# Two attention stages of the second block rewritten: scores from high and low halves on 32-row and 64-row tiles

## The chip, the cores and the metric

The kernel runs on one core of a Trainium2 chip. The metric is the device time of one launch in microseconds (us). The core has five engines that matter here: TensorE (PE), VectorE (DVE), ScalarE (ACT), GpSimd (POOL), and SyncE (SP), which issues the weight loads.

## The reference, cut to what matters

Two transformer blocks of two layers each work on 512 tokens of width 1024. The change touches the second block, which also carries 256 context tokens. In each layer four mixers write a quarter of the width each; two of them are attentions with 4 heads of 64:

```python
# neighbourhood attention: query r,q sees the keys of its window, and all 256 context keys
s_loc = einsum('brqhd,brikhd->bhrqik', qg, k_band) * scale + bias   # outside the window: -inf
s_ctx = einsum('brqhd,blhd->bhrql', qg, k_ctx) * scale
p = softmax(concatenate([s_loc, s_ctx]))
# differential attention: each head has two halves of 32 columns, rotated (rope) for the 512 tokens
p = softmax(q1 @ k1.T * scale) - lam * softmax(q2 @ k2.T * scale)   # over 512 + 256 keys
o = p @ v ; y = rms_norm(o, g) * (1 - lam_init)
```

In layer 0 the 256 context tokens are queries too (over the context keys alone); in layer 1 they only give keys and values. All is float32.

## The kernel before, in words

Each engine has its own instruction list in one fixed order; semaphores join them. Names of work: `("S", u)` is the score tile of unit u. A unit is (kind, layer, head pair j, block q of 128 queries, head h). Kinds are "n" and "d" (the 512 tokens in neighbourhood and differential attention: 16 units a layer) and "nc" and "dc" (context queries: 8 units, layer 0 only).

PSUM has 8 banks: `PB` is a ring of six, taken in turn, whose next taker waits until the last user of that bank is done; `PO` is a ring of two, in which a head pair's output gathers over its query blocks. SBUF rings (`PR` probabilities, `PT` transposed probabilities, `BM` bias tiles, 2 slots, `QR`, `TA`) work the same way.

**Neighbourhood attention** (`B["na", l]`). The keys lie in `KZ`, per head a 128-row tile in which the other head's 64 rows are zero, so a score is a plain 128-row float32 matmul of 512 columns and one of 256. Per unit: PE scores `S` and `Sc`; DVE adds the bias tile with a scalar_tensor_tensor (`na_top`), ACT copies `Sc` beside it, DVE takes the maximum over 768, ACT the exponential, DVE the reciprocal and a multiply of all 768 (`share`); PE transposes (`turn`, 3 units later), ACT copies the transposes (`keys_down`), PE multiplies with V (`values`, 5 units later). `out_proj(2)`, the output projection of the mixer before, is laid between the first units, two of its 8 column tiles at each of iterations 1 to 4. POOL makes the bias tiles in its own loop, in which `fetch(n + 1)` waits until DVE has used tile n - 1 and then issues two DMAs, and the next wait is for the DMAs of tile n:

```python
for n in range(len(us)):
    if n + 1 < len(us):
        fetch(n + 1)
    eng.wait_ge(*after(("bl", us[n])))
    b = S["BM"].get(us[n])
    eng.tensor_tensor(b, b, S["MASK"], ADD).then_inc(*done(("bm", us[n])))
```

**Differential attention** (`B["df", l]`). The head pairs are two sequences, j = 0 then j = 1. For each: PE projects q and k, ACT copies them (`QR`), PE multiplies with the rotation matrix, POOL and DVE join the parts (`rope`), DVE writes k as four zero-padded tiles of 128 rows (`KZ`, 4 additions on 32 rows); only then come the units. Per unit: four score tiles (two halves, each 512 and 256 keys, in a bank each), `df_top` with four reduces, a join and a scaling, `df_one` with four exponentials, `df_share` with a reciprocal, a multiply of 768 and a scalar_tensor_tensor of 768, then `turn`, `keys_down`, `values` as above with lags of 2 and 3. `out_proj(1)` is laid into iterations 1 to 4 of j = 0. After each j: squares, a sum on PE, logarithm and exponential on ACT, three Newton steps and a product on DVE. Then `out_proj(3)`.

The first block's grouped attention (`gqa_score`, `attend_blocks`) already works on pairs of units: high and low halves in the type fp32r, three products on 64-row tiles, the two heads in turn, unscaled probabilities, and one scaling of the output (`shares`, `out_scaled`).

Of the kernel before, what the change touches and what calls it, by code (L numbers as in the profile page):

```python
# [25 lines left out]
F32 = mybir.dt.float32  # L26
# [5 lines left out]
P = 128  # L32
D = 1024
KD = D // P
T = 512
# [48 lines left out]
def constants():  # L84
# [60 lines left out]
    mask = np.where(inside, 0.0, -1e30).astype(f)  # L145
# [99 lines left out]
class Ring:  # L245
# [13 lines left out]

    def get(self, key):  # L260
        known = self.steps.known
        return self.slots[0 if known is None else known[("slot", self.name, key)]]

# [4 lines left out]
def build(nc, A, known):  # L268

    ctx = ExitStack()  # L270
    with ctx:
# [39 lines left out]
        banks = [ctx.enter_context(nc.psum_tensor(f"bank_{i}", [P, 512], F32)) for i in range(8)]  # L311
# [38 lines left out]
        PB = Ring(st, "PB", [b[:, :] for b in banks[0:6]])  # L350
        PO = Ring(st, "PO", [b[:, :] for b in banks[6:8]])
# [125 lines left out]
        def common(c, tag, sq=3, sums=1):  # L477

            return dict(SQ=c.ring("SQ" + tag, sq, T), Y=c.ring("Y" + tag, 2, T), N=c(T), AC=c.ring("AC" + tag, sums, T))
# [3 lines left out]
        def attention(c, tag, nk, p_slots, t_slots):  # L483
            return dict(PR=c.ring("PR" + tag, p_slots, nk), PT=c.ring("PT" + tag, t_slots, nk // P, P),
                        ST=c.ring("ST" + tag, 6, 16))

        def paired(c, tag, nk, p_slots, t_slots):
            return dict(RB=c.ring("RB" + tag, 1, T), RS=c.ring("RS" + tag, 3, 8), PR=c.ring("PR" + tag, p_slots, nk),
# [43 lines left out]
        for l in range(L):  # L532
# [12 lines left out]
            b = dict(H=H, YG=Y2, Q=c(2, T + CT), KZ=c(4, T + CT), V=c(6, 256), MASK=c(T), BM=c.ring("BM" + t, 2, T), **com)  # L545
            b.update(attention(c, t, T + CT, 4, 5))
# [3 lines left out]
            b = dict(H=H, YG=Y2, Q=c(T + CT), KZ=c(4, T + CT), V=c(6, 256), TAB=c(2, T),  # L550
                     QR=c.ring("QR" + t, 1, T), TA=c.ring("TA" + t, 1, T), TBB=c(T), **com)
            b.update(attention(c, t, T + CT, 4, 4))
# [28 lines left out]
        def na_units(l):  # L581
            return units("n", l, range(2), TB) + (units("nc", l, range(2), 2) if l == 0 else [])

        def df_units(l, j):
            return units("d", l, [j], TB) + (units("dc", l, [j], 2) if l == 0 else [])
# [27 lines left out]
        def _(eng):  # L613
# [70 lines left out]
            def turn(u, S, blocks, ready="p"):  # L684

                eng.wait_ge(*after((ready, u)))
                pk = (u, 0) if u[0] in ("d", "dc") else u
                p = S["PR"].get(pk)
# [60 lines left out]
            def attend(us, S, score, V, blocks, okey, nq, between=None, turn_lag=TURN, value_lag=VALUES):  # L749

                for i in range(len(us) + value_lag):
                    if between:
                        between(i)
# [1814 lines left out]
```

## Time and profile before

| | us |
|---|---|
| median of 3 runs (lowest, highest) | 3548.5 (3540.64, 3551.41) |
| the profiled execution, its own time | 3541.35 |
| its span | 3539.6 |
| neighbourhood attention from its first score, layer 0 and 1 | 91.05 and 76.8 |
| differential attention from its first projection to `out_proj(3)`, layer 0 and 1 | 214.75 and 185.4 |

A launch is one pass through the stages. The four stretches in the last two lines are what the change rewrites; their sum is 568 us, 16% of the span. The granted clock of TensorE is given as a share of 2.4 GHz.

### The profile page before, as it was taken

The numbers are of one execution on the slowest core, as the hardware profiler recorded it, in microseconds if no ns is written. First come the engines' busy times: TensorE is split into PE (matmuls) and PEld (weight loads), VectorE is DVE, ScalarE is ACT, GpSimd is POOL, SyncE is SP. The second block draws the span as 40 slices with busy tenths as digits, with TensorE's granted clock in tenths as the row PEclk, the third lists the DMA queues.
The fourth block names the chain that finished last, engine by engine and source line by source line (L and its number), as shares of the span: only waits on it lengthen the run. The fifth ranks groups of instructions, "written<-read, shape, count | busy, mean of one in ns | idle before, by whom it ended". The sixth has DMA issues, their size and how long they took to land.

```text
span 3539.6 us, 38820 instructions
## 1 busy us (share of the span) xinstructions
PE 3237.2 (91%) x15536; PEld 2082.1 (59%) x15536; DVE 1327.0 (37%) x2224; ACT 1012.4 (29%) x1976; POOL 233.2 (7%) x224
## 2 busy tenths in 40 slices
PE   7999979998999979988999878999999998869998
PEld 3555644534555545433666446888788565448886
DVE  2452231223552322121433754333323333563444
ACT  2452211111551211123123444222222222343332
POOL 0010000000000100000022001000001022000000
PEclk9999989998999989998999999999999999989999
DMA  4011238871002248885210001333232210013221
GB/s 165 25 37 49 72 120 356 357 323 50 35 25 78 77 200 336 366 343 211 71 36 25 13 1 72 119 119 119 109 118 76 99 41 26 1 61 105 97 95 48
DMA packets 62001, 413.62 MB, mean 117 GB/s; under 512 B 7504, under 2 KB 8016, under 8 KB 14464
## 3 DMA queue, kind: packets, MB, share of 16 engines
q1 hardware_dynamic: 55664, 392.06, 28.7%
q0 software_dynamic: 5008, 16.98, 1.4%
q8 instruction: 126, 2.06, 0.2%
q10 hardware_dynamic: 1152, 2.10, 0.2%
q14 instruction: 51, 0.42, 0.0%
HBM read 409.01 MB, written 2.10 MB: 116 GB/s over the span
## 4 chain that ended last, share of the span: by engine, by line
PE 85%; DVE 8%; ACT 3%; issue 2%; POOL 1%; DMA 1%; DVEq 0%; ACTq 0%; SPq 0%; POOLq 0%
PE bank L644 82%; PE bank L645 3%; DVE arena L1798 3%; ACT arena L1292 3%; DVE x L1798 1%; DMA weight<-in_ada_w 0%; POOL arena L2471 0%; POOL arena L2481 0%; POOL arena L2413 0%; DVE arena L2031 0%; DVE arena L2333 0%; DVE arena L2029 0%; DVE tokens_low L1798 0%; DMA weight<-in_w_up 0%; DVE arena L2049 0%
## 5 line engine op out<-in xcount | busy, mean ns | idle before, releaser
L644 PE MATMUL bank<-arena,weight 128*128 128x512 f32 (+2 forms) x2080 | 826.4, 555 | 59.1 <-DVE arena L1798 42.0
L1292 ACT ACTIVATE arena<-bank 128x512 f32<-128x512 f32 (+5 forms) x746 | 374.5, 520 | 1690.2 <-PE bank L644 1394.7
L644 PE MATMUL bank<-arena 128*64 128x128 f32 (+4 forms) x3888 | 620.6, 342 | 54.7 <-ACT arena L1292 23.7
L644 PEld LDWEIGHTS bank<-arena,weight 128*128 128x128 f32 (+1 forms) x2080 | 392.7, 191 | 469.9 <-issue 427.5
L644 PE MATMUL bank<-weight,arena 128*64 128x512 f32 (+5 forms) x2936 | 608.8, 530 | 33.0 <-ACT arena L1292 9.7
L644 PEld LDWEIGHTS bank<-arena 128*128 128x128 f32 (+2 forms) x3888 | 399.7, 170 | 238.5 <-issue 142.8
L644 PEld LDWEIGHTS bank<-weight,arena 128*64 128x64 f32 (+2 forms) x2936 | 294.9, 150 | 316.2 <-issue 261.3
L644 PE MATMUL bank<-hidden,weight_part 128*128 128x512 f32 (+1 forms) x2304 | 446.4, 355 | 0.0
L644 PE MATMUL bank<-tokens_high,weight_part 128*128 128x512 f32 (+1 forms) x1536 | 420.6, 359 | 23.9 <-DVE tokens_low L1798 23.7
L644 PEld LDWEIGHTS bank<-hidden,weight_part 128*128 128x128 f32 x2304 | 381.1, 189 | 70.3 <-DVE arena L1798 3.5
L644 PEld LDWEIGHTS bank<-tokens_high,weight_part 128*128 128x128 f32 x1536 | 276.5, 191 | 82.7 <-DVE tokens_low L1798 30.4
L644 PE MATMUL bank<-tokens_low,weight_part 128*128 128x512 f32 (+1 forms) x768 | 274.4, 357 | 0.0
L645 PE MATMUL bank<-mats,arena 128*128 128x128 f32 (+1 forms) x1232 | 176.9, 280 | 69.7 <-DVE arena L1798 26.4
L2413 POOL TENSOR_TENSOR arena<-arena 128x512 f32<-128x512 f32 x72 | 85.0, 1180 | 2098.4 <-ACT arena L1292 2096.7
L1798 DVE SCALAR_TENSOR_TENSOR x<-bank,arena,x 128x512 f32<-128x512 f32 x192 | 142.8, 748 | 200.1 <-PE bank L644 199.5
L645 PEld LDWEIGHTS bank<-mats,arena 128*128 128x128 f32 (+1 forms) x1232 | 143.0, 143 | 127.1 <-DVE arena L1798 44.0
L1292 ACT ACTIVATE weight_part<-weight 128x2048 fp32r<-128x2048 f32 x64 | 122.1, 1908 | 325.6 <-PE bank L644 322.1
L1292 ACT ACTIVATE arena<-bank,arena 128x512 f32<-128x512 f32 (+1 forms) x312 | 185.5, 608 | 71.1 <-DVE arena L2298 49.4
L1798 DVE SCALAR_TENSOR_TENSOR arena<-arena 128x512 f32<-128x512 f32 (+5 forms) x177 | 109.9, 628 | 211.0 <-ACT arena L1292 207.2
L1292 ACT ACTIVATE arena<-arena 128x512 f32<-128x512 f32 (+4 forms) x264 | 163.3, 631 | 66.4 <-DVE arena L2256 40.9
L2357 DVE TENSOR_TENSOR weight_part<-weight,weight_part 128x2048 fp32r<-128x2048 f32 x64 | 146.7, 2292 | 91.6 <-ACT weight_part L1292 88.3
L1834 DVE TENSOR_REDUCE arena<-bank 128x1 f32<-128x512 f32 (+1 forms) x160 | 98.0, 634 | 211.2 <-PE bank L644 207.4
(115 smaller groups left out, 1676.7 us busy)
## 6 DMA issues: line engine op xcount, KB each, us to landing
weight<-in_w_gate SPq DMA_DIRECT2D x64, 1024.0 KB, 13.8
weight<-in_w_up SPq DMA_DIRECT2D x64, 1024.0 KB, 6.7
weight<-in_w_down SPq DMA_DIRECT2D x64, 1024.0 KB, 10.1
weight<-in_w_ff SPq DMA_DIRECT2D x64, 1024.0 KB, 5.0
weight<-in_ada_w SPq DMA_DIRECT2D x48, 1024.0 KB, 5.5
weight<-in_w_in SPq DMA_DIRECT2D x26, 1024.0 KB, 6.1
weight<-in_w_o SPq DMA_DIRECT2D x8, 1024.0 KB, 4.8
weight<-in_w_mem_kv SPq DMA_DIRECT2D x8, 1024.0 KB, 4.8
```

The lines of the kernel that those rows point to most:

```text
L644: mm = lambda o, a, b, first=True, last=True: eng.matmul(o, a, b, start=first, stop=last, skip_group_check=True)
L645: tr = lambda o, a, rows=P: eng.transpose(o, a, mat("ident", rows, rows))
L1292: act = lambda o, i, f=ACT.Copy, **k: eng.activation(o, i, f, **k)
L1798: stt = lambda o, a, s, b, p, q: eng.scalar_tensor_tensor(out=o, in0=a, scalar=s, in1=b, op0=p, op1=q)
L1834: eng.tensor_reduce(s[:, 0:1], PB.get(("S", u))[:, 0:n], AX, MAX, negate=True).then_inc(*done(("nb", u)))
L2357: tt(b, weights[slot_of[key]][:, :], a, SUB).then_inc(*done(("split", key), WF(key)))
L2413: eng.tensor_tensor(a, a, S["SQ"].get((tag, k))[:, 0:n], ADD).then_inc(*done(S["SQ"].free((tag, k)), *((("summed", tag),) if k == KD - 2 e ...
```

## The change

**Scores.** q and k are written as a high part in the type fp32r (`high`, on ACT) and a low part (`low`, on DVE), and a score is the sum of high x high, high x low and low x high. In neighbourhood attention (`na_score`) the two heads of a pair lie in rows 0 to 63 and 64 to 127 and their products follow each other in turn; the loop is `attend_blocks`, in which an iteration is a pair of units and `out_proj(2)` lies in iterations 1 to 4 of these. In differential attention (`df_score`) each half of a head lies in 32 rows, and the six products of one half (512 and 256 keys, three parts) follow each other into two neighbouring banks of `PB` (`take_pair`), so that DVE and ACT read 768 keys at once; the transposes of a unit take such a pair too (`turn_wide`).

**Order.** Both head pairs of differential attention are projected and rotated first, and their units are one sequence. The sums of squares of the first head pair come six iterations after its last unit.

**Softmax.** In neighbourhood attention `tensor_tensor_reduce` adds the bias and takes the minimum of the negated score in one instruction, for 512 and for 256 keys; the probabilities stay unscaled, and the output is divided by the sums (`shares`, `out_scaled`); DVE copies the transposes of each second head. In differential attention `p = p1 + s * p2` needs one pass of 768, and the output is divided afterwards.

POOL's loop over the bias tiles keeps its order, its two slots and its two DMAs a tile. The zero-fills of `KZ` are gone. The diff, cut to its core (PE first, then ACT, DVE and POOL):

```diff
+    def take_pair(self, key):
+
+        self.n += self.n % 2
+        slot = self.n % len(self.slots)
+        self.n += 2
+        formers = [self.free(self.owner[i]) for i in (slot, slot + 1) if i in self.owner]
+        self.owner[slot] = self.owner[slot + 1] = key
+        self.steps.put(("slot", self.name, key), slot)
+        return self.pairs[slot // 2], formers
...
+PB = Ring(st, "PB", banks[0:6])
+PB.pairs = [p[:, :] for p in pairs[0:3]]
...
-    b = dict(H=H, YG=Y2, Q=c(2, T + CT), KZ=c(4, T + CT), V=c(6, 256), MASK=c(T), BM=c.ring("BM" + t, 2, T), **com)
-    b.update(attention(c, t, T + CT, 4, 5))
+    b = dict(H=H, YG=Y2, **{n: c.rounded(f"na_{n}{l}", 2, T + CT) for n in ("QH", "QL", "KH", "KL")}, V=c(6, 256),
+             MASK=com["AC"].slots[0], ZERO=com["AC"].slots[1][:, 0:1], BM=Ring(st, "BM" + t, com["SQ"].slots), **com)
+    b.update(paired(c, t, T + CT, 4, (2, 2), [com["N"]]))
...
-    b = dict(H=H, YG=Y2, Q=c(T + CT), KZ=c(4, T + CT), V=c(6, 256), TAB=c(2, T),
-             QR=c.ring("QR" + t, 1, T), TA=c.ring("TA" + t, 1, T), TBB=c(T), **com)
...
+    b = dict(H=H, YG=Y2, **{n: c.rounded(f"df_{n}{l}", 2, T + CT) for n in ("QH", "QL", "KH", "KL")}, V=c(6, 256), TAB=com["SUMS"],
+             QR=Ring(st, "QR" + t, com["SQ"].slots), TA=c.ring("TA" + t, 1, T), TBB=c(T), **com)
+    b.update(RB=c.ring("RB" + t, 1, T), RS=c.ring("RS" + t, 3, 8), PR=c.ring("PR" + t, 4, T + CT),
+             PT=c.ring("PT" + t, 3, 6, P), ST=c.ring("ST" + t, 6, 8))
...
+    def turn_wide(u, S, blocks):
+
+        eng.wait_ge(*after(("p", u)))
+        p = S["PR"].get((u, 0))
+        o, formers = PB.take_pair(("T", u))
+        for former in formers:
+            eng.wait_ge(*after(former))
+        for c in range(blocks):
+            i = tr(o[:, c * P:(c + 1) * P], p[:, c * P:(c + 1) * P])
+        i.then_inc(*done(("out", ("T", u)), S["PR"].free((u, 0))))
...
-        def na_score(u):
-            kind, _, j, q, h = u
...
-                tile(("S", u), [S["Q"][:, j, q * P:q * P + P]], [z[:, 0:T]])
-                tile(("Sc", u), [S["Q"][:, j, q * P:q * P + P]], [z[:, T:T + CT]], n=CT)
...
-        attend(na_units(l), S, na_score,
...
+        def na_score(pu):
...
+            for name, keys in (("S", slice(0, T)), ("Sc", slice(T, T + CT))):
...
+                o = [take_bank((name, u)) for u in heads_of(pu)]
+                for n, (a, b) in enumerate((("QH", "KH"), ("QH", "KL"), ("QL", "KH"))):
+                    for h in range(2):
+                        r = slice(64 * h, 64 * h + 64)
+                        i = mm(o[h][:, 0:keys.stop - keys.start], S[a][r, j, at:at + P], S[b][r, j, keys], n == 0, n == 2)
...
+        attend_blocks(na_blocks(l), S, na_score,
...
-        def df_score(u):
+        def df_score(u, half):
             kind, _, j, q, h = u
-            for half in range(2):
-                z = S["KZ"][:, 2 * h + half, :]
...
+            o, formers = PB.take_pair(("S", u, half))
+            for former in formers:
+                eng.wait_ge(*after(former))
+            z = 2 * h + half
+            r = slice(32 * z, 32 * z + 32)
...
+            for n, (a, b) in enumerate((("QH", "KH"), ("QH", "KL"), ("QL", "KH"))):
+                lhs = S[a][r, j, at:at + P]
                 if kind == "d":
-                    lhs = [S["Q"][:, q * P:q * P + P]]
-                    tile(("S", u, half), lhs, [z[:, 0:T]])
-                    tile(("Sc", u, half), lhs, [z[:, T:T + CT]], n=CT)
...
+                    mm(o[:, 0:T], lhs, S[b][r, j, 0:T], n == 0, n == 2)
+                c = T if kind == "d" else 0
+                i = mm(o[:, c:c + CT], lhs, S[b][r, j, T:T + CT], n == 0, n == 2)
...
+        project("dq", "w_dq", [0], both, True, wdq)
+        project("dk", "w_dk", [0], True, True, wdk)
+        df_turn("dq", 0)
+        project("dq", "w_dq", [1], both, True, wdq)
+        df_turn("dk", 0)
+        project("dk", "w_dk", [1], True, True, wdk)
+        df_turn("dq", 1)
+        us = df_units(l)
+        for i in range(len(us) + DF_LAG + 1):
+            if i == 0:
+                df_turn("dk", 1)
+            beside(1)(i)
+            if i == len(us) // 2 + DF_POST:
+                df_norm(0)
+            if i < len(us):
+                df_score(us[i], 0)
+            if DF_LAG <= i < len(us) + DF_LAG:
+                u = us[i - DF_LAG]
+                turn_wide(u, S, 6 if u[0] == "d" else 2)
+            if i < len(us):
+                df_score(us[i], 1)
+            if DF_LAG < i and us[i - DF_LAG - 1][4] == 1:
+                u = us[i - DF_LAG - 1]
+                values([u[:4] + (h,) for h in range(2)], S,
...
+                if df_ends(u):
+                    shares(df_okey(u), S, u[3] + 1, 2)
+        df_norm(1)
...
+        def high(dst, key, scale, j, i):
...
+            act(S[dst][:, j, cols], PB.get(key)[:, 0:(T, CT)[i]], scale=scale).then_inc(*done((key[0] + "h", l, j, i)))
...
-        def na_soft(u):
...
-            act(p[:, T:T + CT], PB.get(("Sc", u))[:, 0:CT], ACT.Copy, scale=64 ** -0.5).then_inc(*done(PB.free(("Sc", u)), ("sc", u)))
...
-            act(p, p, ACT.Exp, bias=s[:, 1:2], accum_out=s[:, 2:3]).then_inc(*done(("e", u)))
...
+        def na_exps(pu):
...
+            for u in heads_of(pu):
+                eng.wait_ge(*after(("nb", u)))
+                p, at = S["PR"].get(u), 2 * pu[3] + u[4]
+                src = p if pu[0] == "n" else PB.get(("Sc", u))[:, 0:CT]
+                act(p if pu[0] == "n" else p[:, 0:CT], src, ACT.Exp, bias=S["ST"].get(u)[:, 0:1], scale=-1.0,
+                    accum_out=r[:, at:at + 1]).then_inc(*done(*((PB.free(("Sc", u)),) if pu[0] == "nc" else ()), S["ST"].free(u), ("e", u)))
...
-                    act(p[:, 0:T], PB.get(("S", u, half)), ACT.Exp, bias=b, scale=32 ** -0.5, accum_out=s[:, 6 + 2 * half:7 + 2 * half]).then_inc(*done(PB.free(("S", u, half))))
-                    act(p[:, T:T + CT], PB.get(("Sc", u, half))[:, 0:CT], ACT.Exp, bias=b, scale=32 ** -0.5, accum_out=s[:, 7 + 2 * half:8 + 2 * half]).then_inc(*done(PB.free(("Sc", u, half)), *((("e", u),) if half else ())))
...
-            squares(("od", l, j), S, [PO.get(("od", l, j))])
...
+        def df_exp(u, half):
...
+            act(p[:, 0:n], PB.get_pair(("S", u, half))[:, 0:n], ACT.Exp, bias=s[:, half:half + 1],
+                accum_out=total).then_inc(*done(PB.free(("S", u, half)), ("e", u, half)))
...
+        def df_down(u):
...
+            act(pt[:, 0:n, :], PB.get_pair(("T", u))[:, 0:n * P].rearrange("p (c q) -> p c q", c=n)).then_inc(*done(PB.free(("T", u)), ("pt", u, 0)))
...
+            if i < len(us):
+                df_exp(us[i], 0)
+            if DF_LAG <= i < len(us) + DF_LAG:
+                df_down(us[i - DF_LAG])
+            if i < len(us):
+                df_exp(us[i], 1)
+            if DF_LAG < i and df_ends(us[i - DF_LAG - 1]):
+                u = us[i - DF_LAG - 1]
+                shares(df_okey(u), S, u[3] + 1)
...
+        def low(dst, high, key, scale, j, i):
...
+            stt(S[dst][:, j, cols], PB.get(key)[:, 0:(T, CT)[i]], scale, S[high][:, j, cols], MUL, SUB).then_inc(*done(PB.free(key), (key[0] + "l", l, j, i)))
...
-            stt(p[:, 0:T], PB.get(("S", u)), 64 ** -0.5, S["BM"].get(u), MUL, ADD).then_inc(*done(PB.free(("S", u)), S["BM"].free(u), ("pr0", u)))
...
-            eng.tensor_reduce(s[:, 0:1], p, AX, MAX).then_inc(*done())
-            eng.wait_ge(vector_step, done.count)
-            ts(s[:, 1:2], s[:, 0:1], -1.0, None, MUL).then_inc(*done(("nb", u)))
...
+        def na_tops(pu):
+            for u in heads_of(pu):
...
+                eng.wait_ge(*after(("out", ("S", u))))
+                eng.wait_ge(*after(("bm", u)))
+                eng.tensor_tensor_reduce(p[:, 0:T], PB.get(("S", u)), S["BM"].get(u), 1.0, 3.0e38, ADD, ALU.min,
+                                         s[:, 0:1]).then_inc(*done(PB.free(("S", u)), S["BM"].free(u)))
+                eng.wait_ge(vector_step, done.count)
+                eng.wait_ge(*after(("out", ("Sc", u))))
+                eng.tensor_tensor_reduce(p[:, T:T + CT], PB.get(("Sc", u))[:, 0:CT], S["ZERO"].broadcast_to([P, CT]), 1.0, s[:, 0:1], ADD, ALU.min,
+                                         s[:, 0:1]).then_inc(*done(PB.free(("Sc", u)), ("nb", u)))
...
-                    eng.tensor_reduce(s[:, 2 * half:2 * half + 1], PB.get(("S", u, half)), AX, MAX).then_inc(*done())
...
-                eng.tensor_reduce(s[:, 10:12], s[:, 0:4].rearrange("p (a b) -> p a b", a=2), AX, MAX).then_inc(*done())
-                eng.wait_ge(vector_step, done.count)
-                ts(s[:, 4:6], s[:, 10:12], -(32 ** -0.5), None, MUL).then_inc(*done(("nb", u)))
...
-                eng.reciprocal(s[:, 14:16], s[:, 12:14]).then_inc(*done())
...
-            tt(s[:, 15:16], s[:, 15:16], LAM[l][:, 4:5], MUL).then_inc(*done())
...
-            ts(p, p, s[:, 14:15], None, MUL).then_inc(*done())
-            eng.wait_ge(vector_step, done.count)
-            stt(p, q, s[:, 15:16], p, MUL, ADD).then_inc(*done(("p", u), S["ST"].free(u), S["PR"].free((u, 1))))
...
-                tt(S["KZ"][r, z, 0:T], S["TA"].get(rkey)[r, :], S["TBB"][r, :], ADD).then_inc(*done(*((S["TA"].free(rkey), S["QR"].free(rkey), ("dkc", l, j, 0)) if z == 3 else ())))
...
+            eng.wait_ge(*after(("ta", (l, n, j))))
+            tt(a, a, S["TBB"], ADD).then_inc(*done(("drope", l, n, j), S["QR"].free((l, n, j))))
...
+            tt(low[:, j, 0:T], S["TA"].get((l, n, j)), high[:, j, 0:T], SUB).then_inc(*done((n + "l", l, j, 0), S["TA"].free((l, n, j))))
...
+        def df_top(u, half):
...
+            eng.tensor_reduce(s[:, half:half + 1], PB.get_pair(key)[:, 0:T + CT if u[0] == "d" else CT], AX, MAX, negate=True).then_inc(*done(("nb", u, half)))
...
+        def df_join(u):
...
+            eng.wait_ge(*after(("e", u, 1)))
+            eng.reciprocal(s[:, 3:4], s[:, 2:3]).then_inc(*done())
+            eng.wait_ge(vector_step, done.count)
+            stt(s[:, 4:5], s[:, 3:4], S["RS"].get(df_okey(u))[:, at:at + 1], LAM[l][:, 4:5], MUL, MUL).then_inc(*done())
+            eng.wait_ge(vector_step, done.count)
+            p, q = S["PR"].get((u, 0))[:, 0:n], S["PR"].get((u, 1))[:, 0:n]
+            stt(p, q, s[:, 4:5], p, MUL, ADD).then_inc(*done(("p", u), S["ST"].free(u), S["PR"].free((u, 1))))
...
+        for n, j in tiles4:
+            df_rope(n, j)
+            df_low(n, j)
+        us = df_units(l)
+        for i in range(len(us) + DF_LAG + 2):
+            beside(1)(i)
+            if i < len(us):
+                df_top(us[i], 0)
+            if 1 <= i <= len(us):
+                u = us[i - 1]
+                df_join(u)
+                if df_ends(u):
+                    shares(df_okey(u), S, [])
+            if i == len(us) // 2 + DF_POST:
+                df_post(0)
+            if i < len(us):
+                df_top(us[i], 1)
+            if DF_LAG + 1 < i and df_ends(us[i - DF_LAG - 2]):
+                u = us[i - DF_LAG - 2]
...
-        eng.memset(S["KZ"], 0.0).then_inc(*done(("nz", l)))
...
-            eng.tensor_tensor(b, b, S["MASK"], ADD).then_inc(*done(("bm", us[n])))
+            eng.tensor_tensor(b, S["MASK"], b, SUB).then_inc(*done(("bm", us[n])))
```

`attend_blocks`, `keys_down`, `shares` and `out_scaled` of the first block take the block count and width as arguments now; there they do the same as before.

## Rows read from the trace of the kernel before

**Rows 1.** The page: the chain that ended last, by engine.

```profile
PE 85%; DVE 8%; ACT 3%; issue 2%; POOL 1%; DMA 1%; DVEq 0%; ACTq 0%; SPq 0%; POOLq 0%
```

**Rows 2.** Windows of the four stages: stretch, length, busy time per engine, clock, DMA.

```profile
1814.10:1905.15 91.05, 79.14 (x481) 52.63 (x479) 69.10 (x128) 42.99 (x108) 38.27 (x43) 0.96 0.13 41
1905.15:2119.90 214.75, 175.43 (x802) 112.42 (x801) 114.12 (x278) 75.77 (x233) 8.31 (x6) 0.96 0.02 8
2881.40:2958.20 76.80, 63.23 (x386) 40.05 (x384) 59.30 (x88) 35.78 (x82) 38.30 (x43) 0.96 0.15 49
2958.20:3143.60 185.40, 149.50 (x655) 93.30 (x653) 91.28 (x206) 62.31 (x185) 8.31 (x6) 0.94 0.01 3
```

**Rows 3.** Timeline of differential attention, PE: start, length, work, idle before and releaser.

```profile
1946.62 1.02 PE L644 MATMUL bank<-arena,mats 128*128 128x512 f32 x2
1954.88 5.22 PE L644 MATMUL bank<-arena 128*128 128x512 f32 x8 [3.88 <-DVE arena L2333]
1959.93 5.32 PE L644 MATMUL bank<-arena,weight 128*128 128x512 f32 x16
...
2002.70 2.85 PE L644 MATMUL bank<-arena 128*128 128x512 f32 x8 [1.41 <-ACT arena L1292]
2005.38 0.82 PE L645 MATMUL bank<-mats,arena 128*128 128x128 f32 x6
...
2012.65 1.16 PE L644 MATMUL bank<-arena 128*128 128x256 f32 x4 [1.47 <-ACT arena L1292]
...
2022.00 0.38 PE L645 MATMUL bank<-mats,arena 128*128 128x128 f32 x2
...
2112.42 1.13 PE L644 MATMUL bank<-arena,mats 128*128 128x512 f32 x2
```

**Rows 4.** Timeline of neighbourhood attention, layer 0, one turn of the bias tiles.

```profile
1850.17 0.68 DVE L1798 SCALAR_TENSOR_TENSOR arena<-bank,arena 128x512 f32<-128x512 f32 x1
...
1851.40 1.36 POOL L2471 DMA_DIRECT2D arena<-in_rpb  x2 [1.58 <-DVE arena L1798]
...
1852.77 1.27 POOL L2481 TENSOR_TENSOR arena<-arena 128x512 f32<-128x512 f32 x1
...
1854.39 0.68 DVE L1798 SCALAR_TENSOR_TENSOR arena<-bank,arena 128x512 f32<-128x512 f32 x1
```

**Rows 5.** Timeline of the same stage's start, PE, layer 0, then layer 1.

```profile
1815.38 5.32 PE L644 MATMUL bank<-arena,weight 128*128 128x512 f32 x16
1820.54 1.45 PE L644 MATMUL bank<-arena 128*128 128x512 f32 x4
...
2882.68 3.60 PE L644 MATMUL bank<-arena,weight 128*128 128x512 f32 x8
2886.11 1.45 PE L644 MATMUL bank<-arena 128*128 128x512 f32 x4
```

**Rows 6.** Timeline of the first block's grouped attention, PE: one pair of units.

```profile
158.57 0.50 PE L644 MATMUL bank<-gqa_high 64*128 64x512 f32 x2
...
159.47 1.09 PE L645 MATMUL bank<-mats,arena 128*128 128x128 f32 x8
...
160.49 1.09 PE L644 MATMUL bank<-arena 128*64 128x128 f32 x16
```

**Rows 7.** Groups by form over the whole span: fp32r matmuls of the feed-forward stages.

```profile
L644 PE MATMUL bank<-hidden,weight_part 128*128 128x512 f32 x1536 | 363.0, 391 | 0.0
L644 PE MATMUL bank<-hidden,weight_part 128*128 128x256 f32 x768 | 102.1, 282 | 0.0
```

**Rows 8.** Groups by form of 1754 to 2125 us, DVE and ACT.

```profile
L2254 DVE TENSOR_REDUCE arena<-arena 128x1 f32<-128x768 f32 x16 | 15.2, 953 | 10.4 <-ACT arena L1292 10.4
L1798 DVE SCALAR_TENSOR_TENSOR arena<-arena 128x768 f32<-128x768 f32 x16 | 16.3, 1018 | 0.6
L1292 ACT ACTIVATE arena<-arena 128x768 f32<-128x768 f32 x16 | 15.0, 936 | 20.4 <-DVE arena L2256 20.4
```

**Rows 9.** Windows inside neighbourhood attention, layer 0.

```profile
1864.00:1869.00 5.00, 5.00 (x35) 3.76 (x34) 4.36 (x6) 2.17 (x5) 3.17 (x4) 0.66 0.16 52
```

More of the change, by code:

```diff
@@ L144, in constants @@
     inside = (kc >= start) & (kc < start + 16)
-    mask = np.where(inside, 0.0, -1e30).astype(f)
+    mask = np.where(inside, 0.0, 1e30).astype(f)
     mask = np.tile(mask, (2, ROWS))
@@ L310, in build @@
                          for i, name in enumerate(("tokens_high", "tokens_low", "hidden_0", "hidden_1"))]
-        banks = [ctx.enter_context(nc.psum_tensor(f"bank_{i}", [P, 512], F32)) for i in range(8)]
+        pairs = [ctx.enter_context(nc.psum_tensor(f"banks_{i}", [P, 1024], F32)) for i in range(4)]
+        banks = [pairs[i // 2][:, 512 * (i % 2):512 * (i % 2) + 512] for i in range(8)]
         def mat(name, k=P, m=P):
@@ L704, in values @@
                 for u in us:
-                    for part in range(0, blocks, 4):
+                    for part in range(0, blocks, 4) if u[0] not in ("d", "dc") else (0,):
                         eng.wait_ge(*after(("pt", u, part)))
@@ L1239, in _, with df_turn, df_norm @@
+                    i.then_inc(*done(("out", ("S", u, half))))
+                def df_turn(n, j):
+                    eng.wait_ge(*after(("dqr", l, n, j)))
+                    tile(("drot", l, n, j), [mat("rot_diff")], [S["QR"].get((l, n, j))])
+                def df_norm(j):
                     norm_sums(("od", l, j), S, range(1), 1, "head64", ring=PB)
@@ new lines, in df_down, with df_squares @@
+                def df_down(u):
+                    n = 6 if u[0] == "d" else 2
+                    pt = S["PT"].take(u)
+                    if S["PT"].former:
+                        eng.wait_ge(*after(S["PT"].former))
+                    eng.wait_ge(*after(("out", ("T", u))))
+                    act(pt[:, 0:n, :], PB.get_pair(("T", u))[:, 0:n * P].rearrange("p (c q) -> p c q", c=n)).then_inc(*done(PB.free(("T", u)), ("pt", u, 0)))
+                def df_squares(j):
+                    for i in range(1 + both):
+                        cols = (slice(0, T), slice(T, T + CT))[i]
+                        squares((("od", "odc")[i], l, j), S, [S["YG"][:, j, cols]], (T, CT)[i], lambda k: ("od2", l, j, i))
@@ L2322, in _, with df_rope @@
-                for j in range(2):
-                    if j:
-                        eng.wait_ge(*after(("out", ("od", l, 0))))
-                    rope(("drot", l, "dq", j), (l, "dq", j), S, S["TAB"][:, 1, :], S["Q"][:, 0:T], keys=(("dqc", l, j, 0),))
-                    key, rkey = ("drot", l, "dk", j), (l, "dk", j)
+                tiles4 = [(n, j) for j in range(2) for n in ("dq", "dk")]
+                def df_rope(n, j):
+                    key, a = ("drot", l, n, j), S["TA"].get((l, n, j))
@@ new lines, in df_top @@
+                def df_top(u, half):
+                    if half == 0:
+                        s = S["ST"].take(u)
+                        if S["ST"].former:
+                            eng.wait_ge(*after(S["ST"].former))
+                    s = S["ST"].get(u)
+                    key = ("S", u, half)
+                    eng.wait_ge(*after(("out", key)))
+                    eng.tensor_reduce(s[:, half:half + 1], PB.get_pair(key)[:, 0:T + CT if u[0] == "d" else CT], AX, MAX, negate=True).then_inc(*done(("nb", u, half)))
```

406 lines of the change are left out of this document (155 added, 251 removed).

## The prediction

> **What bounds the kernel now.** I read the page's chain of waits first, for which engine the end hangs on: PE holds 85% of it [rows 1]. An average over all stages says little about four stretches, so the windows of those came next [rows 2]: PE is busy 79.1 of 91.05, 175.4 of 214.75, 63.2 of 76.8 and 149.5 of 185.4 us, DVE 334 of 568 in all, ACT 217. So there are some 101 us in which PE idles, and the question is who makes it idle. The timeline of PE answers for differential attention [rows 3]: a rotation starts at 1946.62 and the first score at 1954.88, so 8.3 us go by with 1.9 us of PE work; then each pair of units takes 9.95 us (2002.70 to 2012.65), and PE idles 1.41 us per unit for ACT, because four score banks and two transpose banks are the whole ring. In neighbourhood attention it is another engine: there the timeline [rows 4] shows DVE using a bias tile at 1850.17, POOL issuing two DMAs (1.36), then adding the mask (1.27), and DVE using the next tile at 1854.39. One unit every 4.22 us, 3.54 of them from one use to the next. Only the first units, with `out_proj(2)` between them, are slower than that: 6.45 us in layer 0, of which 5.2 are the projection, and 3.4 of projection in layer 1 [rows 5].
>
> **Neighbourhood attention, part by part.** PE: six products of 512 columns on two 64-row tiles take 0.90 us in the first block (158.57 to 159.47 in [rows 6]), where two float32 scores take 2 x 0.85 (four scores of 512 and four of 256 take 2.85, [rows 3]). With 0.45 for 256 keys (half of 0.90), 12 transposes at 1.02/8 (1.5) and 12 products with V at 1.09/8 (1.6) [rows 6] a pair of units costs PE 4.45 us where it was about 5.7. DVE: `tensor_tensor_reduce` of 512 replaces a scalar_tensor_tensor of 0.68 [rows 4]; the trace shows no such instruction. Bounds: 0.68 (the same two inputs), and twice that if it takes two passes, 1.36; I take 0.75, near the one-pass row, with a little for giving out the minimum. Gone are a reduce of 768 (0.95, [rows 8]) and a multiply of 768 a unit; they lay beside POOL's chain and are worth nothing. The `KZ` fill and the smaller `low`, `high` copies lie under the projections, 42 us of PE work; without that cover they would cost some 5 us.
>
> POOL's chain isn't touched: 3.54 + 0.75 = 4.29 us a unit, 8.6 a pair, against 4.45 of PE. But the order around it is new. An iteration takes the banks S, S, Sc, Sc, T, T, T, T of a ring of six, so the last transposes of pair i-1 need the bank of the second S of pair i, which DVE frees only when that head's bias tile has come. After that PE still has the last two transposes (0.25), V of pair i-2 (1.6), the projection if there is one (5.2 or 3.4) and the next S (0.9, and 0.1 to signal) before DVE can use the next tile; and the tile after that starts only then. An iteration with projection thus costs 0.25 + 1.6 + 5.2 + 1.0 + 0.75 + 4.29 = 13.1 us in layer 0 and 11.3 in layer 1, and the projection hides nothing of POOL's second tile. Layer 1, ends of each pair's second reduce after the first score starts: 6.0, 14.6, 24.3 (no V yet), 35.6, 46.9, then three at 8.6: 72.7; 6.4 more for exponential, transposes, copy, V and the new `shares` makes 79.1 against 76.8 [rows 2]. Layer 0: 6.0, 14.6, 26.1, 39.2, 52.3, then to 78.1, and some 14 for the context pairs: 92 against 91.05. Sum: **+3.5 us**.
>
> The clock comes on top. TensorE is granted 0.66 in a stretch of this stage [rows 9] that follows idle spells of about 2 us: it spends part of it on the lower of its two levels, 1.2 instead of 2.4 GHz. After the change PE idles 4.1 of 8.6 us. At the low level the 2.75 us between DVE's release and the next S become 5.5, which is 2.0 more than POOL's 3.54. Bounds per pair: 0 and 2.0; I take 1.0 for seven pairs a layer: **+14 us**.
>
> **Differential attention.** The projections (21.0 for V, then 20.8 and 20.65 in layer 0, 17.35 twice in layer 1, read off the same timeline as [rows 3]) stay. The rotations and their 6.4 us of waiting each time now lie under the next projection. What is late next is `TA`, a ring of one: the last two tiles go through it one after the other, rotation, DVE 1.4, ACT 0.65, DVE 0.7, POOL 1.3, DVE 0.7, ACT, DVE, 6.3 us, and DVE's first `df_top` is queued behind them. PE covers part of it with two scores and half a projection step, 2.7 us stay open in layer 0, 1.7 in layer 1.
>
> A half is six products in one 32-row tile, one after the other. fp32r products of 512 and 256 columns come every 0.236 and 0.133 us [rows 7] (363.0/1536 and 102.1/768), so 1.11 us, and 0.19 for going from 128-row to row-tiled work and back (0.90 in [rows 6] less 3 x 0.236): 1.3 us, 2.6 a unit, as much as before. So the gain is not PE work; it is the waits. The Trainium skill, TensorE: Matmul & The Clock Gate, Part 3, says that a single product with 32 rows takes as long as one with 128, and that only tiles running beside each other gain (3.07 times for four). By it nothing would be gained here either, since a half's products share a tile and full-height transposes stand between the halves; were the halves concurrent, a pair of units would cost PE 2.2 us less.
>
> Cycle of two units, from the end of an `exp` of a second half (0): second score 1.35, V to 2.95, next first score 4.25, reduce of 768 (0.95, [rows 8]) 5.3, then the join of the unit before (two small ones of 0.2 and 1.02, [rows 8]) 6.75, the reduce queued behind it 7.75, exponential (0.94 [rows 8] and 0.2 for its sum) 8.95. Nothing of PE's list ends later. So 9.0 us a pair for 9.95. Bounds: 8.45 if a half costs 0.96 (bare columns), 10.3 if a half costs what a float32 one does (2.85/2, [rows 3]) plus 0.19.
>
> Layer 0: projections and four rotations 65.8; first five units with `out_proj(1)` (8.5 an iteration, PE-bound) 39.8; eleven units at 4.5, 49.5; eight context units at 2.4 (9.35 for four, 2012.65 to 2022.00 in [rows 3]) 19.4; sums of the first head pair and `shares` 3.8; tail 13.2, of which 7.5 stood there before (2112.42 to 2119.9) and 1.2 are `shares`, its copy and `out_scaled`: 191.5 against 214.75, **-23.3**. Layer 1: 59.3 + 32.0 + 49.5 + 1.9 + 15.5 = 158.2 against 185.4, **-27.2**.
>
> **Sum.** -50.5 + 3.5 + 14 = -33 us. The profiled execution took 3541.35 us (span 3539.6), 7 us below the median of 3548.5; the three runs span 11 us. -33 from its own time is 3508; from the median, which is what will be measured, 3515.5.
>
> **Rivals.**
> 1. Bias tiles alone pace neighbourhood attention, and the clock holds: if the bank order doesn't bind, 16 tiles at 4.29 and the tails give 75 and 83 us, -10 in all; with the bare-column bound in the other stage -6 more. 3548.5 - 66 = 3482. For it: PE has only 4.45 of work in 8.6. Against: the ring as counted above. Chance 0.12.
> 2. `tensor_tensor_reduce` takes two passes: 0.61 us more for each of 32 tiles, all on the chain: +20. 3535. Against: it reads what the old instruction read. Chance 0.12.
> 3. Slower: PE's idling in neighbourhood attention takes the clock to 1.2 GHz for all of it. Each iteration's PE stretch doubles: +8 for three iterations and 2.0 for three in layer 0, 6.3 and 2.0 in layer 1, 55 us, and 10 in the tails. -50.5 + 3.5 + 65 = +18, 3566. For it: [rows 9], and half the cycle idle. The Trainium skill's TensorE page (Why this matters for your kernels) asks for no idle gaps between bursts, which is this rival's rule; the trace has it in part, 0.66 there and 0.96 over the stage. Against: the projection iterations are dense. It decides from about three quarters of the stage at the low level (47 us). Chance 0.11.
> 4. The two-bank halves don't help: 10.3 us a pair and the clock loss at its upper bound. -33 + 14 + 14 = -5: 3543, no difference. Chance 0.07.
>
> **How the numbers follow.** The forecast (-15 to -50 us, 3498 to 3533) has 0.58. A difference under 0.3%, 11 us, is about what can't be told from none here. Faster by more than that: forecast, rival 1 and half of rival 2, 0.76. Within: the other half and rival 4, 0.13. Slower: 0.11. The range takes in rival 1, rival 2 and most of rival 4: 3483 to 3550.
>
> **What would show it.** In the profile after: bias tiles used 4.3 us apart in pairs, with S of the next pair starting some 2 us after the second of them; neighbourhood attention no shorter than 91 and 77 us, its granted clock below 0.96; DVE's new instruction at 0.7 to 0.8 us; first score of differential attention right behind the last rotation, first reduce some 4 us later; 9 us a pair, with PE waiting under 1 us for ACT or DVE; 190 and 158 us for the stage. The prediction is wrong if a half takes over 1.6 us, if the new DVE instruction is over 1 us, or if PE's clock in neighbourhood attention falls under 0.7.

## The result, and the profile after

The changed kernel takes 3582.48 us (median of 4 runs, 3578.51 to 3589.56), the one before 3547.52 beside it: 1.0103 times as long, 95% interval 1.008 to 1.0125. It is 35 us slower where 33 us less were forecast. The profiled execution took 3581.54 us, its span 3579.8; 40.2 more than the span before.

The page's chain of the span's end, by engine, and then the four stages in the windows of the changed kernel, cut at the same events as [rows 2] (columns: length, busy us and instructions of each engine, granted TensorE clock, DMA share, GB/s). PE holds 86% of the chain, as it did before with 85% [rows 1], so the page alone doesn't tell where the time went:

```profile
PE 86%; DVE 6%; ACT 2%; POOL 2%; issue 2%; DMA 1%; DVEq 0%; ACTq 0%; SPq 0%; POOLq 0%
```

```profile
1812.85:1912.74 99.89, 77.11 (x569) 55.05 (x568) 42.63 (x115) 29.84 (x72) 38.27 (x43) 0.88 0.12 38
1912.74:2150.16 237.42, 218.11 (x931) 152.95 (x929) 94.90 (x177) 71.25 (x155) 5.63 (x5) 0.74 0.02 7
2911.51:2996.15 84.64, 60.88 (x449) 42.47 (x449) 33.45 (x91) 23.72 (x50) 38.26 (x43) 0.86 0.14 44
2996.15:3183.69 187.54, 172.06 (x750) 117.68 (x749) 73.71 (x115) 56.63 (x105) 5.64 (x5) 0.79 0.01 3
```

Neighbourhood attention is 8.8 and 7.8 us longer, 16.7 in all (17.5 forecast). Differential attention is 22.7 and 2.1 longer, where it should have been 23 and 27 shorter. PE is busy 218 of 237 us there, so the waits did go; but the granted clock fell from 0.96 and 0.94 [rows 2] to 0.74 and 0.79. PE's timeline in layer 1, where nothing but this stage's own work is left:

```profile
3096.68 1.54 PE L669 MATMUL banks<-mats,arena 128*128 128x128 f32 x6
3098.15 1.00 PE L668 MATMUL banks<-df_KH,df_QH 32*128 32x512 f32 x2
3098.96 0.84 PE L668 MATMUL banks<-df_KL,df_QH 32*128 32x512 f32 x2
3099.60 0.84 PE L668 MATMUL banks<-df_KH,df_QL 32*128 32x512 f32 x2
3100.36 2.83 PE L668 MATMUL banks<-arena 128*64 128x128 f32 x24
...
3114.09 2.83 PE L668 MATMUL banks<-arena 128*64 128x128 f32 x24
```

None of these lines has idle time in brackets. A half goes from 3098.15 to 3100.36, 2.2 us, and a pair of units from 3100.36 to 3114.09, 13.7 us, where I had 1.3 and 9.0. Two windows (the columns are those of the windows above): first a stretch of layer 0 with `out_proj(1)` still between the units, then the stretch just shown:

```profile
2003.00:2027.00 24.00, 23.94 (x112) 15.13 (x110) 14.42 (x24) 8.14 (x16) 0.00 (x0) 0.93 0.13 44
...
3100.36:3127.82 27.46, 27.46 (x122) 21.23 (x121) 13.01 (x21) 10.74 (x20) 0.00 (x0) 0.50 0.00 1
```

0.50 is the lower of the two levels, 1.2 GHz, granted while PE is busy 27.46 of 27.46 us. In the first stretch a half takes 1.25 us, near the 1.3 forecast (it starts at 2010.36, and the transposes behind it at 2011.61). In neighbourhood attention the timeline shows the wait for the bank ring that the prediction had counted:

```profile
1865.44 1.43 PE L669 MATMUL banks<-mats,arena 128*128 128x128 f32 x10
1870.24 0.69 PE L669 MATMUL banks<-mats,arena 128*128 128x128 f32 x2 [3.36 <-DVE arena L2292]
```

The last two transposes stand 3.36 us for a bank that DVE's instruction with the bias tile frees. The two tiles of a pair are used 4.08 us apart (1865.40 and 1869.48 on DVE) where 4.29 were counted. That instruction is as costly as taken, 0.69 us and 0.08 for its result (groups of DVE in that stage):

```profile
L2292 DVE CUSTOM_DVE_ANT_0 arena<-banks,arena 128x512 f32<-128x512 f32 x16 | 11.1, 692 | 53.6 <-PE banks L668 32.4 <-POOL arena L2513 20.1 <-PE banks L669 1.1
...
L2292 DVE DVE_READ_ACCUMULATOR2_ANT arena<- 128x1 f32 x16 | 1.3, 83 | 0.0
```

### The profile page after: what moved, and what is told of

It is laid out like the page before. It is cut to its first block, busy times and chain, and to the rows that moved or that the text cites. A ratio compares the mean times of both kernels' runs of the same rounds, so it can differ in the third digit from the quotient of the medians.

```text
span 3579.8 us, 39391 instructions
## 1 busy us (share of the span) xinstructions
PE 3296.0 (92%) x15912; PEld 2151.3 (60%) x15912; DVE 1246.7 (35%) x2038; ACT 973.5 (27%) x1742; POOL 222.7 (6%) x220
## 4 chain that ended last, share of the span: by engine, by line
PE 86%; DVE 6%; ACT 2%; POOL 2%; issue 2%; DMA 1%; DVEq 0%; ACTq 0%; SPq 0%; POOLq 0%
PE banks L668 83%; PE banks L669 4%; DVE arena L1842 3%; ACT arena L1345 2%; POOL arena L2503 1%; DMA weight<-in_w_up 1%; POOL arena L2513 1%; DVE x L1842 0%; DMA weight<-in_ada_w 0%; POOL arena L2447 0%; DVE arena L2051 0%; DVE arena L2049 0%; DVE tokens_low L1842 0%; DVE arena L2069 0%; DVE arena L2338 0%
## 5 line engine op out<-in xcount | busy, mean ns | idle before, releaser
L668 PE MATMUL banks<-arena,weight 128*128 128x512 f32 (+2 forms) x2080 | 839.2, 561 | 55.5 <-DVE arena L1842 43.9
L1345 ACT ACTIVATE arena<-banks 128x512 f32<-128x512 f32 (+4 forms) x606 | 329.4, 554 | 1530.7 <-PE banks L668 1336.4
L668 PEld LDWEIGHTS banks<-arena,weight 128*128 128x128 f32 (+1 forms) x2080 | 396.8, 194 | 476.4 <-issue 439.5
L668 PE MATMUL banks<-weight,arena 128*64 128x512 f32 (+5 forms) x2936 | 608.7, 529 | 33.8 <-ACT arena L1345 9.7
L668 PE MATMUL banks<-arena 128*64 128x128 f32 (+3 forms) x3456 | 482.7, 338 | 18.8 <-DVE arena L2069 11.8
L668 PEld LDWEIGHTS banks<-weight,arena 128*64 128x64 f32 (+2 forms) x2936 | 295.5, 151 | 316.7 <-issue 263.2
L668 PE MATMUL banks<-hidden,weight_part 128*128 128x512 f32 (+1 forms) x2304 | 446.4, 355 | 0.0
L668 PE MATMUL banks<-tokens_high,weight_part 128*128 128x512 f32 (+1 forms) x1536 | 420.5, 359 | 24.0 <-DVE tokens_low L1842 23.9
L668 PEld LDWEIGHTS banks<-hidden,weight_part 128*128 128x128 f32 x2304 | 381.0, 189 | 70.3 <-issue 3.5
L668 PEld LDWEIGHTS banks<-arena 128*64 128x64 f32 (+2 forms) x3456 | 336.4, 176 | 136.4 <-issue 102.5
```

The source lines that it names most:

```text
L668: mm = lambda o, a, b, first=True, last=True: eng.matmul(o, a, b, start=first, stop=last, skip_group_check=True)
L1345: act = lambda o, i, f=ACT.Copy, **k: eng.activation(o, i, f, **k)
```

## Experiments

Theory A: products over 32 rows are what takes TensorE's clock down in the dense part. B: it is their type, or the density of three short products in a row. C: waits and ring order make the stage long. The kernel before took 3545 us (medians 3544.8 to 3545.4) beside these runs; each ratio is to it.

**d_alone.** The old neighbourhood attention in the changed kernel.

> Differential attention as after the change, neighbourhood attention as before it. The trace after puts +17 us on neighbourhood attention and +25 us on differential attention, of +35 measured in all. If the two parts add up, this kernel is 17 us below the changed one, about 3565, and still slower than before. Rival: the two stages disturb each other (rings, clock carried over from one stage to the next), and one alone gives something else, 3548 or less or 3582.

3566.8 us, 1.006 (1.0048 to 1.0072). That is 15.7 us under the changed kernel and 22 over the one before; the trace had 17 and 25 for the two stages. The parts add up within 3 us.

**rows128, rows64.**

```diff
-                    r = slice(32 * z, 32 * z + 32)
+                    r = slice(0, P)                    # rows64: slice(64 * h, 64 * h + 64)
```

These two kernels don't compute the reference: a score is summed over four halves, or over two. The run `padded` below computes it.

> The changed kernel, but each score product of differential attention takes all 128 rows instead of 32 (so it sums over four halves and the scores are others; number, type, columns and order of all instructions are the same). Theory A, the height: with 32-row products TensorE is granted 1.2 GHz in the dense part of the stage although it never idles there. Then with 128 rows the clock holds, a half takes 1.25 us throughout, and the stage falls from 237 and 187 to about 195 and 162 us: 3582 - 65 = 3517. Theory B, the type or the density of the three-product scores: height is no matter, the half stays at 2.2 us in the dense part and the time at 3582. Theory C, waits and ring order make the stage long: also 3582.

> As the run with 128 rows, with 64 rows for each score product. Theory A: if the clock depends on the height by degrees, the time lies between 3517 and 3582, with a shorter low stretch than at 32 rows. Theories B and C: 3582.

3524.0 us at 128 rows, 0.9939 (0.9927 to 0.9951); 3544.2 at 64 rows, 0.9999 (0.999 to 1.0007). The stage falls from 237.4 and 187.5 us (32 rows) to 220.0 and 167.6 (64), and to 203.0 and 163.7 (128). PE's windows of the 128-row run: both stages, then the densest part of layer 1.

```profile
1915.40:2118.38 202.98, 175.52 (x931) 126.43 (x929) 93.77 (x177) 70.95 (x155) 5.63 (x5) 0.93 0.03 9
2965.11:3128.80 163.69, 141.76 (x750) 99.41 (x749) 72.99 (x115) 56.53 (x105) 5.62 (x5) 0.95 0.01 4
...
3057.97:3083.68 25.71, 22.97 (x181) 18.87 (x180) 19.31 (x32) 16.57 (x33) 0.00 (x0) 1.00 0.00 1
```

The numbers of instructions are those of the changed kernel, (x931) and (x750), and PE idles more, 2.7 of 25.7 us, yet it is granted 1.00. Six units take 25.7 us, 8.6 a pair. Height alone is worth 58 us; B and C, which gave 3582 for this run, are out as the main cause.

Going to a row tile and back also costs time, and 128-row products save it: at the upper clock transposes and the way to the next product take 0.80 us with 32 rows (2011.61 to 2012.41 in the changed kernel) and 0.57 with 128 (3060.61 to 3061.18 here). Where PE is the bound at that clock, an iteration with `out_proj(1)`, it makes 8.75 us (2010.36 to 2019.11) into 8.55 (2004.38 to 2012.93), so little of the 58 us is that.

With 64 rows there are as many row tiles and as many changes between them and full height, but the clock isn't held down everywhere:

```profile
3090.00:3120.00 30.00, 28.48 (x212) 21.18 (x211) 21.52 (x35) 20.10 (x38) 0.00 (x0) 1.00 0.00 1
...
2050.00:2080.00 30.00, 29.56 (x135) 22.14 (x132) 17.20 (x32) 13.28 (x31) 0.00 (x0) 0.59 0.00 1
```

The first window is in layer 1, where the stage is nearly as short as with 128 rows, the second in layer 0, where it keeps half of the loss. So the changes of tile alone don't explain the low clock. Why 64 rows get 1.00 in one place and 0.59 in the other stays open.

**float32_rows32.** Of the three products only the first, read as float32:

```diff
+                        if n:
+                            continue
-                        lhs = S[a][r, j, at:at + P]
+                        lhs = S[a][r, j, at:at + P].bitcast(F32)   # and the keys likewise
```

> The changed kernel, but each score of differential attention is one float32 product over the same 32 rows instead of three fp32r ones (the low parts are left out of the product, so scores are a little coarser; the float32 product of 512 and 256 columns takes about as long as the three together, 1.4 us at 2.4 GHz). Theory A, the 32 rows take the clock down: the dense stretches run at 1.2 GHz as before, 3582 or a little over. Rival B, it is the fp32r type: the clock holds, 3525 to 3535.

3606.8 us, 1.0177 (1.016 to 1.0194). A half in the last units of layer 0, then the clock of that stretch, which takes in context units:

```profile
2122.78 2.92 PE L668 MATMUL banks<-df_KH,df_QH 32*128 32x512 f32 x4
2125.63 1.54 PE L669 MATMUL banks<-mats,arena 128*128 128x128 f32 x6
...
2120.00:2147.00 27.00, 26.20 (x129) 18.00 (x128) 9.56 (x22) 8.64 (x22) 0.00 (x0) 0.50 0.00 1
```

So neither the type nor three short products in a row is it: 32 rows get 0.50 with one float32 product too. That it would take "about as long as the three together" was a miss: at this clock the half takes 2.85 us (2122.78 to 2125.63) for 2.2, and the run is 24 us slower than the changed kernel, where none or little was expected.

**beside.** Both bank pairs are taken first, then each product of half 0 is followed by that of half 1.

```diff
+                    pairs = [PB.take_pair(("S", u, half)) for half in range(2)]
...
+                            for half in range(2):
+                                r = slice(32 * (2 * h + half), 32 * (2 * h + half) + 32)
+                                i = mm(pairs[half][0][:, c:c + w], S[a][r, j, at:at + P], S[b][r, j, k:k + w], n == 0, n == 2)
```

> The changed kernel with the two halves of a unit issued in turn, product by product, in two 32-row tiles at once (two bank pairs for the scores, then one for the transposes). Theory A: the products run two at a time and twice the rows are at work; if that holds the clock, a unit takes ACT's and DVE's chain, 4.3 us, and the stage 190 and 160 us: 3582 - 50 = 3530. If the clock is as low as before, the concurrency alone takes 2.2 us off a unit of 6.85 in the low stretches: 3582 - 30 = 3550. Theory C, that waits set the time and not TensorE: the scores of a unit now wait for both bank pairs, and it is no faster than 3582.

3558.1 us, 1.0034 (1.0022 to 1.0046): 24 us better than the change, 28 short of A's first number (3530) and 8 short of its second, for concurrency at a low clock (3550). Two units of its timeline, from layer 1:

```profile
3101.28 0.62 PE L668 MATMUL banks<-df_KH,df_QH 32*128 32x512 f32 x4
3101.74 0.51 PE L668 MATMUL banks<-df_KL,df_QH 32*128 32x512 f32 x4
3102.09 0.51 PE L668 MATMUL banks<-df_KH,df_QL 32*128 32x512 f32 x4
3102.53 0.88 PE L669 MATMUL banks<-mats,arena 128*128 128x128 f32 x6
3105.82 0.61 PE L668 MATMUL banks<-df_KH,df_QH 32*128 32x512 f32 x4 [2.42 <-ACT arena L1342]
...
3107.91 2.83 PE L668 MATMUL banks<-arena 128*64 128x128 f32 x24
```

The concurrency is there: four products stand where two stood, and both halves take 1.25 us together. But PE now waits 2.42 us for ACT, and the products with V behind it run at the lower clock (2.83 us for 24, against 1.53 at the upper level). Height and idle time are mixed here, so this run doesn't weigh them.

**padded.** The 128 rows in a kernel that computes the reference. POOL copies a half's 32 query rows, high and low, into zero-filled tiles that lie where `H` was; the keys are used whole.

```diff
+                        z = ring.take((u, half))
+                        r = slice(32 * (2 * h + half), 32 * (2 * h + half) + 32)
+                        for a, name in enumerate(("QH", "QL")):
+                            i = eng.tensor_copy(z[r, a, :], S[name][r, j, at:at + P])
```

> The changed kernel with score products of differential attention over all 128 rows, now computing the reference: POOL copies the 32 rows of the high and low query tile of each half into zero-filled tiles (four small copies a unit, two slots for each of the four positions), and the keys are used whole. Theory A (the height of the products takes the clock down): the time of the run with 128 rows, 3524, since POOL idles in this stage; by the copies being late at the start of the stage, up to 5 us more. Rival: POOL's copies of 32 rows at over 1 us each pace a unit (4 us against 4.3): then 3540 or more.

3530.1 us, 0.9961 (0.9947 to 0.9974): the copies are late once a layer, some 6 us, and PE waits under 1 us for them after that.

**bm3.**

```diff
-BM=Ring(st, "BM" + t, com["SQ"].slots)
+BM=Ring(st, "BM" + t, com["SQ"].slots + [c(T)])
```

> The changed kernel with three slots for bias tiles in neighbourhood attention instead of two; nothing else. My reading: POOL issues the load of tile n+1 only after DVE has used tile n-1, and adds the mask to tile n behind it, so two slots give 4.3 us a tile, 8.6 a pair, and the bank ring makes it 13.1 and 11.3 with a projection. With a third slot POOL runs ahead (2.65 us of its own work a tile), an iteration falls to PE's work, 9.7 and 8 with projection and about 6 without: 20 us less a layer, 3540. Rival D: the bank ring or ACT is what paces it and the tile only came last: 3575 to 3582. Rival E: PE idles less and the clock rises too: 3530.

3528.8 us, 0.9958 (0.9943 to 0.9972): 54 us less than the change, more than the 42 forecast, and neighbourhood attention accounts for it:

```profile
1814.77:1886.88 72.11, 66.37 (x569) 47.66 (x568) 42.46 (x115) 29.27 (x72) 35.68 (x40) 1.00 0.15 49
2885.59:2945.51 59.92, 52.96 (x450) 37.01 (x449) 33.19 (x91) 23.27 (x50) 35.63 (x40) 0.97 0.19 58
```

99.9 and 84.6 became 72.1 and 59.9 us, and PE's busy time fell by 10.7 and 7.9 us for the same work, since the clock rose from 0.88 and 0.86 to 1.00 and 0.97. E holds; D is out.

**before_bm3.** The same slot in the kernel before the change.

> The kernel before the change with a third slot for bias tiles, nothing else. It asks what the rebuilt neighbourhood attention is worth once the tiles don't pace it. Theory: PE's old work is 5.7 us for a pair of units and 5.2 for a projection step, ACT has two copies, two exponentials and more in each unit, near 3 us, so a pair takes 6.2 us or a little over instead of 8.4: some 15 us less a layer, 3545 - 28 = 3517. Then the rebuild with three slots (70 us for layer 0) is ahead by only some 5 to 8 us a layer. Rival: ACT and DVE with 3.5 us of work a unit already pace the old order, and it gains under 8 us in all.

3541.4 us, 0.9991 (0.9982 to 1.0): 4 us where 28 were expected, so the rival's number holds. DVE's timeline of that run shows why, with POOL's mask addition in it and one later multiply of DVE for comparison:

```profile
1862.55 0.68 DVE L1798 SCALAR_TENSOR_TENSOR arena<-bank,arena 128x512 f32<-128x512 f32 x1
...
1863.75 0.95 DVE L2254 TENSOR_REDUCE arena<-arena 128x1 f32<-128x768 f32 x1 [0.52 <-ACT arena L1292]
...
1864.99 1.89 DVE L1884 TENSOR_SCALAR arena<-arena 128x768 f32<-128x768 f32 x1
1865.17 1.28 POOL L2481 TENSOR_TENSOR arena<-arena 128x512 f32<-128x512 f32 x1
...
1866.81 0.68 DVE L1798 SCALAR_TENSOR_TENSOR arena<-bank,arena 128x512 f32<-128x512 f32 x1
...
1885.18 0.62 DVE L1884 TENSOR_SCALAR arena<-arena 128x768 f32<-128x768 f32 x1
```

DVE's own round through a unit is 4.26 us (1862.55 to 1866.81) with POOL's tile long ready. Its multiply takes 1.89 us while POOL adds the mask, and 0.62 at 1885.18, with POOL done: 0.62 and POOL's 1.28 make 1.90, as if one ran after the other. In the kernel before it was the same, and DVE, not POOL, came last. The rows show it [rows 4]: POOL's addition ends at 1854.04, and DVE uses the tile at 1854.39, right behind this:

```profile
1852.61 1.86 DVE L1884 TENSOR_SCALAR arena<-arena 128x768 f32<-128x768 f32 x1
```

So before the change two loops of nearly one length ran there: DVE's of 4.2 us, and POOL's, which takes 4.08 for the two tiles of a pair in the changed kernel. The change shortened one, the third slot the other. The third slot alone gives 4 us and the change alone loses 16.7; both together gain 18.9 and 16.9 us a layer against [rows 2].

**padded_bm3.** The edits of `padded` and `bm3` together.

> Both: products over 128 rows with zero-filled query tiles, and three slots for bias tiles. If both hold and add up: 3582 - 58 - 42 = 3482, below the kernel before and the changed one. If only the height holds: 3520.

3478.5 us, 0.9816 (0.9801 to 0.983): the two add up, within 4 us.

**padded_bm3_post.** The middle of the sequence in PE's timeline of `padded_bm3`:

```profile
2048.33 0.82 PE L672 MATMUL banks<-mats,arena 128*128 128x128 f32 x6
2054.99 0.98 PE L671 MATMUL banks<-df_KH,df_QZ 128*128 128x512 f32 x2 [5.84 <-DVE arena L1844]
```

```diff
-                    if i == len(us) // 2 + DF_POST:
+                    if i == len(us) + 1:        # PE, ACT and DVE; ACT's squares at len(us)
```

> The version with 128-row products and three bias slots; the sums of squares, roots and scaling of the first head pair's output are moved from the middle of the unit sequence to just behind its last unit. In the middle PE waits 5.8 us in layer 0 and 4.7 in layer 1 for the banks that these sums hold, and works at 1.2 GHz for some 3 us after it. Theory: that is saved, and the tail grows by at most 3 us a layer, since DVE's 2.7 us of it lie beside PE's last products: 3478.5 - 8 = 3470. Rival: the tail is serial and grows by as much as was saved: no change.

3464.2 us, 0.9772 (0.9757 to 0.9786): 14 us less where 8 were expected. The stage fell from 205.5 and 167.6 to 198.1 and 161.5 us; the tail hid the moved work.

**padded_bm3_early.**

> As the run before it, and the first four units of differential attention take their scores straight from the 32 rows, so that they don't wait for the zero-fill and the first copies of POOL (PE waits 6.1 and 6.2 us there). Theory: 12 us less than the run before it, 3458, and the clock isn't taken down, since out_proj(1) lies between these units. Rival A2: four units of 32-row products are enough to lower the clock at that place and give half of it back: 3464. Rival: the first reduce can't start earlier anyway because DVE's own last tile ends there: no change.

3462.5 us, 0.9764 (0.9751 to 0.9778): not to be told from the run before, so the 12 us expected aren't there, and rival A2's 3464 fits as well as no change does. In layer 1 the first score comes 8 us earlier in the stage, but PE then waits 3.74 us for `df_KL` before the second, and the units take 85 instead of 79 us at 0.88 and 0.97 where they had 0.89 and 1.00. How the loss splits between DVE's late tile and the clock stays open.

## Why the prediction was wrong

**The step that failed** is the cost of differential attention's units: "Nothing of PE's list ends later. So 9.0 us a pair for 9.95". It took the half at 1.3 us, transposes and products with V from rows at 2.4 GHz. The half is right at that clock (1.25). But the list runs without a gap at 1.2 GHz, 2.2 us a half and 13.7 a pair, and PE becomes the bound. I had priced the clock only where PE idles. With 128 rows and the same instructions otherwise the stage is 34.4 and 23.8 us shorter: these 58 us turn +25 into -33.5. The Trainium skill, TensorE: Matmul & The Clock Gate, Why this matters for your kernels, asks for no idle gaps; this trace shows that their absence isn't enough, with 0.50 granted at 27.46 busy of 27.46 us.

**What the forecast still lacked:** -33.5 is not -50.5. The pair came out better (8.6 for 9.0). Two terms were too small. For the first head pair's sums and `shares` it had 3.8 and 1.9 us; moving the sums out of the middle, where PE waits 5.84 us in layer 0, gave 14. And the eight context units of layer 0 were put at 19.4 us, from the old order. In the 128-row run the first four take 14.0 us (from their first score to that of the unit behind them), and the other four 13.6, from 2089.55 to the end of their last score:

```profile
2034.71 0.36 PE L668 MATMUL banks<-df_KH,df_QH 128*128 128x256 f32 x1 [0.64 <-ACT arena L1345]
...
2048.74 0.59 PE L668 MATMUL banks<-df_KH,df_QH 128*128 128x512 f32 x2 [0.45 <-DVE arena L1842]
```

That is some 8 us for each of the two terms, less 4 for the shorter pairs: about 12 of the 17 missing. The rest is not traced to a cause.

**Neighbourhood attention** came out near the forecast, +16.7 for +17.5, with the order of banks, the 0.75 for `tensor_tensor_reduce` and a clock of 0.88 and 0.86, between the levels. Some of the closeness is luck: a tile came 4.08 us after the one before it and not 4.29, so the rest took more than was counted. Rival 1 (tiles alone, clock held) and rival 2 (two passes) are out. So is rival 4: a pair of differential attention takes 13.7 us at 1.2 GHz and 8.6 with 128 rows, not 10.3. Two sentences were wrong beside a right sum. That DVE's reduce and multiply "lay beside POOL's chain and are worth nothing" takes the wrong engine for the last one: they were part of a second loop that was as long, and POOL's addition lengthened it. The rebuild as a whole, with a third slot, is worth 36 us there; what those two instructions have in it no run separates. And "four scores of 512 and four of 256" in [rows 3] are two of each, since each of the four products that a unit issues is recorded twice (x8); the 0.85 and the 2.85/2 taken from it are right.

**Rival 3** had the right sign and the right engine, the clock at 1.2 GHz, but the wrong stage and condition: idling in neighbourhood attention. Neither rival nor forecast asked what a busy PE would be granted with a quarter of its rows. The balance: -33 forecast, +58 for the 32 rows, nearly all of it clock, +17 for what differential attention lacked beside that, -1 in neighbourhood attention, -1 elsewhere: +40, the difference of the spans.

## What to carry to other kernels

Before moving dense matmul work to low row tiles, run one version with the full height over the same instructions, and read the granted clock of a window in which PE doesn't idle: a price read at 2.4 GHz need not hold. Filling the other 96 rows with zeros cost PE no time in the products and gave 52 us back. Where two engines' loops have about one length, test the removal of both before one is called worthless: the rebuilt neighbourhood attention (+16.7 us alone) and a third slot (-4 alone) gave -36 together. With these repairs the kernel takes 3464 us, 2.3% less than before.

## What the runs showed of the hardware that I had not expected

- TensorE was granted 0.50 over 27.46 us without idle time, with 32-row score products in fp32r, and 0.50 over 27 us with float32 ones; with 128 rows 1.00 over 25.7 us, though PE idled 2.7 of them. With 64 rows both occur, 1.00 and 0.59 over 30 us. The whole stage of layer 0 took 237, 220 and 203 us with 32, 64 and 128 rows.
- Products in two 32-row tiles, issued in turn, run beside each other: two halves in 1.25 us at the upper clock, as long as one alone.
- `tensor_tensor_reduce` of 512 columns costs DVE 0.69 us and 0.08 for its result, one pass.
- A `tensor_scalar` of 768 columns on DVE took 0.62 us with POOL idle and 1.87 to 2.06 us where POOL's addition of 512 columns (1.28 us) fell into its time.
